# The gates' low parts multiplied on GpSimd instead of VectorE, with two buffers of the one-hots that it reads

## The chip, the cores and the metric

One core of one Trainium2 chip. The metric is the time of one execution on the device in microseconds, the median of several runs.

## The reference, cut to what matters

The program is a two-block transformer on 512 tokens of width 1024. The change lies in the first block's expert layer, `peer_ffn`: each token and head picks 16 of 128 x 128 = 16384 experts, each named by a pair of key numbers, and a softmax over the picks' scores gives gates.

```python
q = (xi @ w_q).reshape(n, PEER_HEADS, 2, PEER_KEY_DIM)
s = jnp.einsum('nhpc,hpkc->nhpk', q, sub_keys)
ts, ti = lax.top_k(s, PEER_TOPK)
...
idx = jnp.take_along_axis(cand_i, best_p, axis=-1)
gate = jax.nn.softmax(best_s, axis=-1)
act = gelu(jnp.einsum('nd,nhkd->nhk', xi, u[idx]))
return jnp.einsum('nhk,nhkd->nd', gate * act, v[idx])
```

## The kernel before, in words

Each engine has a program of its own (`TensorProgram`, `ScalarProgram`, `VectorProgram`, `PoolProgram` for GpSimd, `SyncProgram` for DMAs), written out by hand in the order in which the engine runs it. They meet through semaphores: `.up(...)` counts one up when an instruction has finished, `wait_ge(*signal.at(...))` waits for it. An engine does nothing else while it waits.

Of the 512 tokens, 384 (`DT`) go through the expert layer densely: TensorE multiplies them with all 16384 rows of `u` and of `v`, in 128 tiles of 128 experts, and a matrix of gates, zero for experts that a token did not pick, is multiplied in between. The other 128 tokens (one tile, `ROW_TILE`) are done by rows: for each of their 128 picks GpSimd asks for the picked row of `u` or `v` by an indirect DMA (`ask`, L2649 to L2660), into one of four slots (`ROW_SLOTS`), and VectorE takes the dot product (L2219) or adds the row to a sum (L2232); that is `VectorProgram.rows`, and it counts `row_used` up. There are 256 such requests, numbered i by `ROW_USES`; request i waits until row i - 4 is used.

Numbers of high precision are split into two bf16 parts, and TensorE multiplies high with high, low with high and high with low (L564 to L566). Blocks of weights (128x4096) are loaded by Sync, their high part is made by ScalarE (L1289) and their low part by VectorE (`low_part`, L2003) or, outside the expert layer's stretch, by GpSimd in pieces of 512 columns (L2565).

The matrix of gates is built in the loop of `gate_matrices`, 48 steps (`HOT_STEPS = DT // OC`) of 8 tokens each (`OC`), in two buffers by n % 2:

- VectorE (L2369 to L2393) makes the one-hots of the first key number, `one_hot_a` (L2385), and of the second, `one_hot_b` (L2388; one buffer). It multiplies the latter by the gates' high part (L2390) and low part (L2391) into `gated_one_hot_b` 0 and 1; the last counts `hot` up. All are bf16, 128x1024. Between steps it works on rows up to `ROWS_HOT[n]` (three rows in four steps) and on low parts of weights up to `LOWS_HOT[n]` (nine 128x4096 blocks between 849.5 and 1052 us). `one_hot_a` waits until TensorE has used its buffer (`gate_mats`, step n - 2).
- TensorE (L956 to L969) waits for `hot`, multiplies the one-hots (L967, 16 products of 128x128x128 per step), and then runs the dense tiles of `HOT_FILL[n]`, three in four steps, each of 24 products over 384 columns.
- ScalarE (L1603) copies the result (L1613), Sync stores it, and both serve the dense tiles between.
- GpSimd is in `ask` the whole time, ahead of the loop, through it and long after it; `run` calls it once, at L2606.

After the loop TensorE does 12 more dense tiles (`LAST_FILL`) and then the second half of the layer, `experts`.

Of the kernel before, what the change touches and what calls it, by code (L numbers as in the profile page):

```python
# [8 lines left out]
BF16 = mybir.dt.bfloat16  # L9
U32 = mybir.dt.uint32  # L10
ALU = mybir.AluOpType
# [3 lines left out]
P = 128  # L15
# [16 lines left out]
PH, NK, TOPK = 8, 128, 16  # L32
# [9 lines left out]
OC, OI = 8, 2  # L42

ROW_TILE, DT = QT - 1, SEQ - P
ROW_SLOTS = 4
# [41 lines left out]
class Signals:  # L87


    def __init__(self, nc, reached):  # L90
# [69 lines left out]
        self.hot = self.new("one_hots_ready")  # L160
# [42 lines left out]
class Layout:  # L203


    def __init__(self, nc, n_columns):
        m = Map(nc, nc.sbuf_base)
# [27 lines left out]
        m = Map(nc, after_gla)  # L235
        self.norm1 = NormBuffers(m, "norm1", T)
        self.h0 = m("tokens_in", [P, KT, T])
        m = Map(nc, after_gla)
        self.z, self.logit = m("z", [2 * GLA_RANK, T]), m("gate_logit", [P, 4, T])
        self.soft, self.ones_row = m("gate_soft", [P, 4, T]), m("ones_row", [P, T])  # L240
        m = Map(nc, free)
# [25 lines left out]
        self.left, self.right = hot("one_hot_a", one_hots, BF16), hot("one_hot_b", one_hots[:1] + one_hots[2:], BF16)  # L267
# [269 lines left out]
class TensorProgram:  # L537
# [418 lines left out]
    def gate_matrices(self):  # L956
        nc, s, k, m = self.nc, self.s, self.k, self.m
        for n in range(DT // OC):
            v = n % 2
            nc.tensor.wait_ge(*s.hot.at(n))  # L960
            for q in range(OC // 4):
                event = ("gate_mats", n, q)
                i = self.take(event, (s.act_out, event))
                for x in range(4):
                    for part in range(2):
                        c, y = divmod(4 * q + x, OI)
                        ins = nc.tensor.matmul(k.psum[:, i, NK * x:NK * (x + 1)], m.left[:, v, c, :, y],  # L967
                                               m.gated[part][:, v, c, :, y], start=part == 0, stop=part == 1)
                ins.then_inc(*s.gate_mats.up(n, q))  # L969
            self.fill(HOT_FILL[n])  # L970
# [832 lines left out]
class VectorProgram:  # L1803
# [565 lines left out]
    def gate_matrices(self):  # L2369
# [8 lines left out]
        for n in range(HOT_STEPS):  # L2378
            v, tokens = n % 2, slice(OC * n, OC * (n + 1))
            number_a, number_b, gate_high, gate_low = (  # L2380
                m.pick_b[:, x, tokens].rearrange("p (c n) -> p c n", n=OI).unsqueeze(2).to_broadcast(hots)
                for x in range(4))
# [3 lines left out]
            if n >= 1:  # L2386
                nc.vector.wait_ge(*s.hot.at(n - 1))
            nc.vector.tensor_tensor(m.right[:, :, :, :], iota, number_b, ALU.is_equal).then_inc(*s.step.up())  # L2388
            nc.vector.wait_ge(*s.step.now())
            nc.vector.tensor_tensor(m.gated[0][:, v], m.right[:, :, :, :], gate_high, ALU.mult).then_inc(*s.step.up())  # L2390
            nc.vector.tensor_tensor(m.gated[1][:, v], m.right[:, :, :, :], gate_low, ALU.mult).then_inc(*s.hot.up(n))  # L2391
# [160 lines left out]
class PoolProgram:  # L2552
# [19 lines left out]
    def run(self):  # L2572
# [33 lines left out]
        self.ask()  # L2606
# [42 lines left out]
    def ask(self):  # L2649
# [4 lines left out]
        for i, (kind, h, x) in enumerate(ROW_USES):  # L2654
# [241 lines left out]
```

## Time and profile before

| | |
|---|---|
| median of 3 runs | 2268.46 us (2267.76 to 2269.29) |
| profiled execution, its own time | 2262.53 us |
| its span | 2261.2 us |
| mean granted clock of TensorE | 0.972 of full |
| TensorE / VectorE / ScalarE / GpSimd busy | 2109.3 / 1524.8 / 890.9 / 713.0 us |
| GpSimd, 256 requests for rows | 80.5 + 100.4 + 95.6 + 93.6 us |
| GpSimd, weight splits L2565 | 299.5 us in 229 pieces |
| loop of gate matrices | 849.5 to 1052 us |

In the profile PE is TensorE, DVE VectorE, ACT ScalarE, POOL GpSimd and SP Sync. Times are microseconds, unless a column says ns. A group of instructions shows its busy time and the mean of one, then the idle time of its engine ahead of it and what ended that. A stretch shows how long each engine was busy in it, PEclk, the TensorE clock that was granted (1.00 is full speed, 0.50 half), the share of the DMA engines and what they moved. Records of one engine may overlap by their fixed ends, so the distance from start to start tells the pace better than a duration.

### The profile page before, as it was taken

Reading aid. Unit: us, or ns where it says so; the run is one execution under the profiler, and the core shown is the slowest. Engines: PE = TensorE matmul, PEld = TensorE weight load, DVE = VectorE, ACT = ScalarE, POOL = GpSimd, SP = SyncE. Lnnn points to the kernel's source line nnn. Section 1 sums busy time; section 2 is a strip of 40 time slices with the busy share of each in tenths; the row PEclk is TensorE's granted clock in tenths of the full one; section 3 lists DMA queues with packets and bytes.
Section 4 is the critical chain, followed back from the end, with each engine's and each line's share of the span. In section 5 each row is a group of like instructions: output and inputs, shape, how many; then the busy total and the mean of one; then the engine's idle time right before and its main releaser. Section 6 shows DMA issues by size and latency. Waiting matters only on the chain.

```text
span 2261.2 us, 31215 instructions
## 1 busy us (share of the span) xinstructions
PE 2109.3 (93%) x12667; PEld 1220.4 (54%) x12743; DVE 1524.8 (67%) x2558; ACT 890.9 (39%) x1066; POOL 713.0 (32%) x540
## 2 busy tenths in 40 slices
PE   6999889899999988999999999999789898999998
PEld 5464554455556646666665555555445464444444
DVE  4557664698889899998688888888674374432002
ACT  5333553333333336765433333333232454434110
POOL 2311001310333442232233333434336301555440
PEclk9999889999999999999999999999799998999999
DMA  5223552215988878899999999999422201322410
GB/s 207 75 75 114 197 203 83 84 49 195 330 307 299 333 274 300 332 353 341 372 373 378 376 382 377 382 382 374 174 75 98 75 20 38 112 83 104 149 38 37
DMA packets 194478, 483.37 MB, mean 214 GB/s; under 512 B 10672, under 2 KB 93648, under 8 KB 188320
## 3 DMA queue, kind: packets, MB, share of 16 engines
q1 hardware_dynamic: 154624, 334.65, 41.5%
q0 software_dynamic: 39712, 146.74, 17.2%
q8 instruction: 100, 1.64, 0.3%
q14 instruction: 42, 0.34, 0.0%
HBM read 428.92 MB, written 52.43 MB: 213 GB/s over the span
## 4 chain that ended last, share of the span: by engine, by line
PE 48%; DVE 29%; DMA 14%; issue 3%; ACT 3%; POOL 1%; SPq 1%; DVEq 0%; ACTq 0%; POOLq 0%
PE psum L565 13%; PE psum L566 13%; PE psum L564 13%; DMA expert_act<-act_dram 12%; DVE weight_low L2003 6%; DVE row_sum L2232 2%; POOL weight_low L2565 1%; DVE hidden_low L2411 1%; DVE gated_one_hot_b L2391 1%; DVE one_hot_b L2388 1%; DVE one_hot_a L2385 1%; DVE expert_act L2406 1%; DVE rows_a L2219 1%; PE psum L758 1%; PE psum L779 1%
## 5 line engine op out<-in xcount | busy, mean ns | idle before, releaser
L564 PE MATMUL psum<-x_high,weight_high 128*128 128x384 bf16 (+3 forms) x1826 | 630.0, 345 | 21.1 <-DVE weight_low L2003 15.7
L565 PE MATMUL psum<-x_low,weight_high 128*128 128x384 bf16 (+3 forms) x1845 | 637.2, 345 | 12.1 <-DVE x_low L1881 5.9
L566 PE MATMUL psum<-x_high,weight_low 128*128 128x384 bf16 (+3 forms) x1844 | 636.5, 345 | 0.6
L1289 ACT ACTIVATE weight_high<-weight_stage 128x4096 bf16<-128x4096 f32 (+2 forms) x100 | 356.3, 3564 | 240.8 <-PE psum L566 118.1
L2565 POOL TENSOR_TENSOR weight_low<-weight_stage,weight_high 128x512 bf16<-128x512 f32 (+1 forms) x229 | 299.5, 1341 | 422.7 <-ACT weight_high L1289 422.7
L564 PE MATMUL psum<-hidden_high,weight_high 128*128 128x384 bf16 x1024 | 333.8, 326 | 6.3 <-DVE hidden_low L2411 6.2
L566 PE MATMUL psum<-hidden_high,weight_low 128*128 128x384 bf16 x1024 | 333.8, 326 | 0.0
L565 PE MATMUL psum<-hidden_low,weight_high 128*128 128x384 bf16 x1024 | 333.8, 326 | 0.0
L2003 DVE TENSOR_TENSOR weight_low<-weight_stage,weight_high 128x4096 bf16<-128x4096 f32 x69 | 304.6, 4416 | 11.0 <-ACT weight_high L1289 11.0
L564 PEld LDWEIGHTS psum<-x_high,weight_high 128*128 128x128 bf16 (+1 forms) x1856 | 183.3, 99 | 183.1 <-issue 20.5
L566 PEld LDWEIGHTS psum<-x_high,weight_low 128*128 128x128 bf16 (+1 forms) x1856 | 183.4, 99 | 154.1 <-issue 7.0
L565 PEld LDWEIGHTS psum<-x_low,weight_high 128*128 128x128 bf16 (+1 forms) x1856 | 183.3, 99 | 144.4 <-issue 5.5
L1562 ACT ACTIVATE norm_value<-psum 128x384 f32<-128x384 f32 x128 | 62.1, 490 | 297.2 <-PE psum L566 225.0
L2659 POOL DMA_INDIRECT rows_a<-u_rows_dram,row_index x64 | 80.5, 1258 | 287.5 <-DVE rows_a L2219 195.5
L2659 POOL DMA_INDIRECT rows_b<-u_rows_dram,row_index x64 | 100.4, 1569 | 174.5 <-DVE rows_b L2219 168.1
L2659 POOL DMA_INDIRECT rows_b<-peer_v_dram,row_index x64 | 95.6, 1493 | 146.7 <-DVE row_sum L2232 131.8
L564 PEld LDWEIGHTS psum<-hidden_high,weight_high 128*128 128x128 bf16 x1024 | 100.1, 98 | 75.9 <-issue 9.5
L2659 POOL DMA_INDIRECT rows_a<-peer_v_dram,row_index x64 | 93.6, 1462 | 145.1 <-DVE row_sum L2232 135.3
L566 PEld LDWEIGHTS psum<-hidden_high,weight_low 128*128 128x128 bf16 x1024 | 100.2, 98 | 66.2
L565 PEld LDWEIGHTS psum<-hidden_low,weight_high 128*128 128x128 bf16 x1024 | 100.2, 98 | 64.5
L1633 ACT ACTIVATE hidden_high<-expert_act 128x384 bf16<-128x384 f32 x128 | 61.5, 522 | 160.2 <-DVE expert_act L2406 160.2
L2406 DVE TENSOR_TENSOR expert_act<-expert_act,gates 128x384 f32<-128x384 f32 x128 | 62.9, 553 | 74.8 <-DMA expert_act<-act_dram 74.8
(350 smaller groups left out, 2926.3 us busy)
## 6 DMA issues: line engine op xcount, KB each, us to landing
weight_stage<-peer_u_dram SPq DMA_DIRECT2D x32, 2048.0 KB
weight_stage<-peer_v_dram SPq DMA_DIRECT2D x32, 2048.0 KB
weight_stage<-mlp_w_dram SPq DMA_DIRECT2D x16, 2048.0 KB
weight_stage<-ada_w_dram SPq DMA_DIRECT2D x12, 2048.0 KB
act_dram<-norm_value SPq DMA_DIRECT2D x128, 192.0 KB
gate_dram<-gate_matrices SPq DMA_DIRECT2D x12, 2048.0 KB, 9.9
gates<-gate_dram SPq DMA_DIRECT2D x32, 768.0 KB
expert_act<-act_dram SPq DMA_DIRECT2D x32, 768.0 KB
```

The costliest lines, as they stand in the source:

```text
L564: self.nc.tensor.matmul(out, left[0], right[0], start=first, stop=False)
L565: self.nc.tensor.matmul(out, left[0], right[1], start=False, stop=False)
L566: return self.nc.tensor.matmul(out, left[1], right[0], start=False, stop=last)
L758: ins = nc.tensor.matmul(k.psum[strip, i, :], m.cond[:, t, :], rows[:, t, :], start=t < 4, stop=t >= 4)
L1289: nc.scalar.activation(k.block_view(m.w_high, n % SPLITS, n), k.block_view(m.w_stage, n % STAGES, n), ACT.Copy).then_inc(*s.w_high.up(n))
L1562: nc.scalar.activation(m.norm2.value[:, tile % 4, 0:DT], k.tile_bank(event, DT), ACT.Gelu).then_inc(*s.activated.up(*event))
L1633: nc.scalar.activation(m.hid_high[:, n % 2, b, :], m.act[:, n % 2, b, :], ACT.Copy).then_inc(*s.hid_high.up(n, b))
L2003: nc.vector.tensor_tensor(k.block_view(m.w_low, n % SPLITS, n), k.block_view(m.w_stage, n % STAGES, n), k.block_view(m.w_high, n % SPLITS, ...
L2232: nc.vector.scalar_tensor_tensor(m.row_sum[:, :], row, m.row_weight[:, at], m.row_sum[:, :], ALU.mult, ALU.add).then_inc(*s.row_used.up(i))
L2406: nc.vector.tensor_tensor(v, v, m.gates[:, n % 2, :, b, :], ALU.mult).then_inc(*s.gated.up(n, b))
L2565: ins = nc.gpsimd.tensor_tensor(m.w_low[:, n % SPLITS, at], m.w_stage[:, n % STAGES, at], m.w_high[:, n % SPLITS, at], ALU.subtract)
L2659: nc.gpsimd.indirect_dma_start(m.rows[i % ROW_SLOTS], None, v if layer else u, index).then_inc(*s.in_rows[i % ROW_SLOTS].up(i))
```

## The change

VectorE makes `one_hot_b` in two buffers and counts the new signal `right_hot` up; it no longer multiplies by the low part, and its product with the high part now counts `hot` up. GpSimd makes the product with the low part (`PoolProgram.gate_matrices`) and counts `gated_low` up. TensorE waits for both. VectorE waits for `gated_low` of step n - 2 before it writes `one_hot_b` again. GpSimd's requests are cut into parts: those up to `ROWS_ROUTE[-1] + 4` ahead of the loop, then after each product those up to `ROWS_HOT[n] + 3`, and the rest after the loop. In `Layout` the second buffer moves `gated_one_hot_b` and what lies behind it 2 KB per partition up.

```diff
--- before.py
+++ after.py
@@ -157,7 +157,8 @@
         self.softening = self.new("gates_softening")
         self.added = self.new("residual_added")
         self.routed = self.new("experts_chosen")
-        self.hot = self.new("one_hots_ready")
+        self.hot, self.right_hot = self.new("one_hots_ready"), self.new("one_hots_b_ready")
+        self.gated_low = self.new("gated_low_ready")
         self.rescaled = self.new("second_sums_scaled")
         self.summed = self.new("squares_added")
         self.gated = self.new("hidden_gated")
@@ -264,7 +265,7 @@
         self.tot = m("gate_sum", [P, 2, PH])
         hot = Map(nc, top)
         one_hots = [P, 2, OC // OI, NK, OI]
-        self.left, self.right = hot("one_hot_a", one_hots, BF16), hot("one_hot_b", one_hots[:1] + one_hots[2:], BF16)
+        self.left, self.right = hot("one_hot_a", one_hots, BF16), hot("one_hot_b", one_hots, BF16)
         self.gated = [hot(f"gated_one_hot_b_{part}", one_hots, BF16) for part in range(2)]
         mats = hot.at
         self.mats = hot("gate_matrices", [P, 2, NK, TC])
@@ -958,6 +959,7 @@
         for n in range(DT // OC):
             v = n % 2
             nc.tensor.wait_ge(*s.hot.at(n))
+            nc.tensor.wait_ge(*s.gated_low.at(n))
             for q in range(OC // 4):
                 event = ("gate_mats", n, q)
                 i = self.take(event, (s.act_out, event))
@@ -2377,18 +2379,17 @@
         iota = m.iota[:, :, :].unsqueeze(1).to_broadcast(hots)
         for n in range(HOT_STEPS):
             v, tokens = n % 2, slice(OC * n, OC * (n + 1))
-            number_a, number_b, gate_high, gate_low = (
+            number_a, number_b, gate_high = (
                 m.pick_b[:, x, tokens].rearrange("p (c n) -> p c n", n=OI).unsqueeze(2).to_broadcast(hots)
-                for x in range(4))
+                for x in range(3))
             if n >= 2:
                 nc.vector.wait_ge(*s.gate_mats.at(n - 2, OC // 4 - 1))
             nc.vector.tensor_tensor(m.left[:, v], iota, number_a, ALU.is_equal).then_inc(*s.step.up())
-            if n >= 1:
-                nc.vector.wait_ge(*s.hot.at(n - 1))
-            nc.vector.tensor_tensor(m.right[:, :, :, :], iota, number_b, ALU.is_equal).then_inc(*s.step.up())
-            nc.vector.wait_ge(*s.step.now())
-            nc.vector.tensor_tensor(m.gated[0][:, v], m.right[:, :, :, :], gate_high, ALU.mult).then_inc(*s.step.up())
-            nc.vector.tensor_tensor(m.gated[1][:, v], m.right[:, :, :, :], gate_low, ALU.mult).then_inc(*s.hot.up(n))
+            if n >= 2:
+                nc.vector.wait_ge(*s.gated_low.at(n - 2))
+            nc.vector.tensor_tensor(m.right[:, v], iota, number_b, ALU.is_equal).then_inc(*s.right_hot.up(n))
+            nc.vector.wait_ge(*s.right_hot.at(n))
+            nc.vector.tensor_tensor(m.gated[0][:, v], m.right[:, v], gate_high, ALU.mult).then_inc(*s.hot.up(n))
             self.rows(ROWS_HOT[n])
             self.low_parts(LOWS_HOT[n])
 
@@ -2603,7 +2604,7 @@
         nc.gpsimd.dma_start(m.iota32[:, :], d["iota_keys"]).then_inc(*s.in_iota_keys.up())
         for g in range(4):
             self.begin(("peer_q", g))
-        self.ask()
+        self.gate_matrices()
         self.begin(("v", NG - 1))
 
         nc.gpsimd.wait_ge(*s.added.at("experts", KT - 1))
@@ -2646,12 +2647,32 @@
                                 rv[:, :, mid:mid + 1].to_broadcast([P, SEQ // n, n]), ALU.subtract).then_inc(
             *s.gla_step.up(i))
 
-    def ask(self):
+    def gate_matrices(self):
+
+        nc, s, m = self.nc, self.s, self.m
+        asked = ROWS_ROUTE[-1] + ROW_SLOTS
+        self.ask(0, asked)
+        nc.gpsimd.wait_ge(*s.routed.at("split", ROUTE_TILES[-1]))
+        for n in range(HOT_STEPS):
+            v, tokens = n % 2, slice(OC * n, OC * (n + 1))
+            gate_low = m.pick_b[:, 3, tokens].rearrange("p (c n) -> p c n", n=OI).unsqueeze(2).to_broadcast(
+                [P, OC // OI, NK, OI])
+            nc.gpsimd.wait_ge(*s.right_hot.at(n))
+            if n >= 2:
+                nc.gpsimd.wait_ge(*s.gate_mats.at(n - 2, OC // 4 - 1))
+            nc.gpsimd.tensor_tensor(m.gated[1][:, v], m.right[:, v], gate_low, ALU.mult).then_inc(*s.gated_low.up(n))
+            until = ROWS_HOT[n] + ROW_SLOTS - 1
+            self.ask(asked, until)
+            asked = max(asked, until)
+        self.ask(asked, len(ROW_USES))
+
+    def ask(self, first, end):
 
         nc, s, k, m = self.nc, self.s, self.k, self.m
         u, v = k.d["u_rows"], k.d["peer_v"].rearrange("b a n -> (b a) n")
         nc.gpsimd.wait_ge(*s.routed.at("row_lists"))
-        for i, (kind, h, x) in enumerate(ROW_USES):
+        for i in range(first, end):
+            kind, h, x = ROW_USES[i]
             pick, layer = TOPK * h + x, int(kind == "sum")
             if i >= ROW_SLOTS:
                 nc.gpsimd.wait_ge(*s.row_used.at(i - ROW_SLOTS))
```

## Rows read from the trace of the kernel before

**Rows 1.** The page: the span, and the engines' busy time, share and instructions.
```profile
span 2261.2 us, 31215 instructions
...
PE 2109.3 (93%) x12667; PEld 1220.4 (54%) x12743; DVE 1524.8 (67%) x2558; ACT 890.9 (39%) x1066; POOL 713.0 (32%) x540
```

**Rows 2.** Busy time of each engine by stretch; the first column is its length.
```profile
core 0: us, PE busy (x) PEld busy (x) DVE busy (x) ACT busy (x) POOL busy (x), PEclk, DMA share, GB/s
...
900.00:950.00 50.00, 47.05 (x412) 32.20 (x411) 49.60 (x62) 34.43 (x37) 17.35 (x9) 1.00 0.91 350
...
1052.00:1100.00 48.00, 48.00 (x300) 28.96 (x298) 25.58 (x21) 19.64 (x21) 11.50 (x7) 1.00 0.95 340
1100.00:1600.00 500.00, 493.72 (x3032) 295.71 (x3030) 422.41 (x481) 174.12 (x162) 193.92 (x141) 1.00 1.03 373
...
849.50:1052.00 202.50, 185.04 (x1607) 127.86 (x1608) 198.40 (x256) 137.16 (x140) 56.05 (x36) 0.98 0.89 334
```

**Rows 3.** Groups of instructions, 849.5 to 1052 us: busy, mean ns | idle before.
```profile
L967 PE MATMUL psum<-gated_one_hot_b,one_hot_a 128*128 128x128 bf16 x767 | 53.0, 223 | 18.7 <-DVE gated_one_hot_b L2391 18.7
...
L2003 DVE TENSOR_TENSOR weight_low<-weight_stage,weight_high 128x4096 bf16<-128x4096 f32 x9 | 39.8, 4419 | 0.0
...
L2388 DVE TENSOR_TENSOR one_hot_b<-iota_bf,picks_t_bf 128x1024 bf16<-128x1024 bf16 x48 | 33.2, 691 | 0.0
...
L2391 DVE TENSOR_TENSOR gated_one_hot_b<-one_hot_b,picks_t_bf 128x1024 bf16<-128x1024 bf16 x48 | 32.8, 684 | 0.0
...
L2232 DVE SCALAR_TENSOR_TENSOR row_sum<-rows_a,modulation_rows,row_sum 128x1024 f32<-128x1024 f32 x9 | 11.5, 1279 | 0.0
```

**Rows 4.** Timeline, the first products of the loop on TensorE.
```profile
852.21 1.89 PE L967 MATMUL psum<-gated_one_hot_b,one_hot_a 128*128 128x128 bf16 x16 [3.96 <-DVE gated_one_hot_b L2391]
```

**Rows 5.** Timeline of VectorE, the low product and what follows it: start, us, instruction.
```profile
880.14 0.69 DVE L2391 TENSOR_TENSOR gated_one_hot_b<-one_hot_b,picks_t_bf 128x1024 bf16<-128x1024 bf16 x1
880.74 4.42 DVE L2003 TENSOR_TENSOR weight_low<-weight_stage,weight_high 128x4096 bf16<-128x4096 f32 x1
```

**Rows 6.** The view of line L2391: ns min/median/max, first and last start.
```profile
L2391 DVE TENSOR_TENSOR gated_one_hot_b<-one_hot_b,picks_t_bf x48: 682/684/686, 851.5 to 1049.3; 128x1024 bf16<-128x1024 bf16 x48
```

**Rows 7.** Timeline of GpSimd and of VectorE beside it, 420 us.
```profile
420.12 8.96 POOL L2565 TENSOR_TENSOR weight_low<-weight_stage,weight_high 128x512 bf16<-128x512 f32 x8 [5.25 <-ACT weight_high L1289]
...
422.46 0.29 DVE L2198 MAX8 best_side<-scores 128x8 f32<-128x128 f32 x1 [6.88 <-ACT scores L1585]
```

**Rows 8.** Timelines in the loop: GpSimd's requests, and VectorE beside the last.
```profile
896.52 1.15 POOL L2659 DMA_INDIRECT rows_a<-u_rows_dram,row_index  x1 [2.53 <-DVE rows_a L2219]
902.78 4.88 POOL L2659 DMA_INDIRECT rows_a<-peer_v_dram,row_index  x1 [5.12 <-DVE row_sum L2232]
...
902.43 4.42 DVE L2003 TENSOR_TENSOR weight_low<-weight_stage,weight_high 128x4096 bf16<-128x4096 f32 x1
```

**Rows 9.** Timelines of GpSimd and VectorE, the convolution.
```profile
1675.00 12.65 POOL L2565 TENSOR_TENSOR weight_low<-weight_stage,weight_high 128x512 bf16<-128x512 f32 x8 [25.94 <-ACT weight_high L1289]
...
1701.03 28.45 POOL L2565 TENSOR_TENSOR weight_low<-weight_stage,weight_high 128x512 bf16<-128x512 f32 x8 [1.68 <-ACT weight_high L1289]
...
1701.03 20.65 POOL L2565 TENSOR_TENSOR weight_low<-weight_stage,weight_high 128x512 bf16<-128x512 f32 x1 [1.68 <-ACT weight_high L1289]
...
1699.39 21.28 DVE L2441 SCALAR_TENSOR_TENSOR norm_square<-conv_padded,columns,norm_square 128x512 f32<-128x512 f32 x32
```

**Rows 10.** The MLP: GpSimd's timeline for one block; the view of VectorE's L2540.
```profile
1938.46 10.75 POOL L2565 TENSOR_TENSOR weight_low<-weight_stage,weight_high 128x512 bf16<-128x512 f32 x8 [7.16 <-ACT weight_high L1289]
...
L2540 DVE TENSOR_TENSOR norm_square<-norm_square x32: 692/1216/1642, 1922.5 to 2078.6; 128x512 f32<-128x512 f32 x32
```

**Rows 11.** Busy time by stretch, TensorE alone: length, busy, granted clock, DMA share, GB/s.
```profile
255.00:300.00 45.00, 36.78 (x237) 0.92 0.61 210
...
1860.00:1911.00 51.00, 40.50 (x257) 0.89 0.12 42
1624.00:1648.00 24.00, 18.27 (x76) 0.72 0.38 156
```

## The prediction

> **What bounds the kernel now.** The page comes first. TensorE is busy for 93% of the span, VectorE for 67%, GpSimd for 32% [rows 1]; such averages do not say what the touched loop waits for. The busy time by stretch does: in the loop of gate matrices (849.5 to 1052 us) VectorE is busy 198.40 of 202.50 us, and 49.60 of 50 in a stretch of its middle, TensorE only 185.04 and 47.05 [rows 2]. So there VectorE sets the pace. After it the roles change: TensorE is busy 48.00 of 48 us and then 493.72 of 500, VectorE 25.58 and 422.41 [rows 2]. Time lost or won by TensorE in the loop is therefore not made up later; it reaches the end whole, but for some 6 us.
>
> The groups of the loop [rows 3] show the work of its 48 steps: four bf16 operations over 128x1024 per step, 36 expert rows (1.2 to 1.3 us), 9 splits of weights (4.42 us). TensorE sat idle 18.7 us, all of it for the product with the low parts, L2391, and 3.96 us of that ahead of the first step [rows 3, 4]. That leaves 14.7 us: the most that any relief of VectorE can give.
>
> VectorE's timeline gives the price of one operation on the path [rows 5]: L2391 starts at 880.14 and its follower at 880.74, so 0.60 us, not the 0.69 of its record. The 48 runs of L2391 start between 851.5 and 1049.3 us [rows 6], so a step takes VectorE 197.8 / 47 = 4.21 us.
>
> **The change part by part.**
> (1) VectorE drops 48 of L2391: 48 x 0.60 = 28.8 us less.
> (2) GpSimd gains 48 two-input products over 1024 columns. No row has it with bf16 on both sides. Its nearest row is its own weight split, two inputs, 512 columns: 8 in 8.96 us, 1.12 each, while VectorE ran MAX8 and the like, with one tensor input [rows 7]. Twice the columns: 2.24 us. Bounds: 1.12, if two bf16 inputs go at twice the rate, and 2.8, if the gates' repeated pairs and a cold start of every single piece cost a quarter more. I take 2.24, since the row is the same operation. The 36 requests in the loop take GpSimd 56.05 us [rows 2], mostly 1.15 each [rows 8]. 48 x 2.24 + 56 = 164 of 202 us: as a sum of its own it fits.
> (3) What decides is whether GpSimd's product can run beside VectorE. Nearly all that VectorE does in the loop reads two tensors from SBUF (all groups of VectorE in [rows 3], and the product with the high part like its twin L2391). Three places show such work meeting GpSimd's. In the convolution VectorE's 32 L2441 alone take 21.28 us, 0.665 each, and a GpSimd piece that came amid them ended after 20.65 us, when they were through; the same 8 pieces took 28.45 us [rows 9]. A little earlier 8 pieces and VectorE's stream took turns: 12.65 us, 1.58 per piece [rows 9]. In the MLP, 8 pieces take 10.75 us in place of 8.96, and VectorE's L2540, a product of two inputs, goes from 0.69 to a median of 1.22 and up to 1.64 us [rows 10]. In the loop itself a request of GpSimd took 4.88 us, not 1.15, when it came at 902.78 in a weight split of 4.42 us that had begun at 902.43 [rows 8]. So the two take turns. One turn costs 1.58 where VectorE's alone costs 0.665: GpSimd's piece of 1.12 adds 0.915, all but 0.2.
> Then one product adds 2.24 - 0.2 = 2.04 us to VectorE's step and takes 0.60 away: 4.21 + 1.44 = 5.65 us. **Sum: 48 x 1.44 = +69 us.**
> The Trainium skill (SBUF — State Buffer, SBUF: two separate sides) calls the shared port pair an exclusive lock that the winner keeps for its whole instruction; nothing would then overlap, and the sum would be 48 x 1.64 = +79 us. I keep the 0.2 that the alternating rows show.
> (4) The second buffer of one_hot_b takes away VectorE's wait for its own product; that never cost anything here (L2388 shows 0.0 idle [rows 3]). In its place L2388 waits for GpSimd's product of two steps before, and behind it in VectorE's queue stand the product with the high part, which TensorE needs, the rows and the splits. If GpSimd is kept out while VectorE streams, as in the 20.65 us case, this wait and that of one_hot_a for TensorE are what stop VectorE, at most two steps ahead; GpSimd goes in, TensorE takes its 16 products (53.0 / 48 = 1.1 us [rows 3]), and the count per step is again the two engines' work one after the other. So whoever wins the port, the sum is nearly the same; if GpSimd waits for VectorE to stop, some of its product lies beside that stop, and I take 3 us off for the whole loop.
> (5) Requests for rows now stand behind the products. At step n GpSimd asks up to ROWS_HOT[n] + 3, three rows beyond those that VectorE works on in that step, so four steps ahead (three rows per four steps): 4 x 5.6 = 22 us less a lag of up to two steps, 11 us. The wait for a used row is always met by then. A request of 1.15 us and a transfer must fit in 11 us; requests come at 0.75 per step with 3.4 us free for them, so I cost it at nothing. If it is late VectorE idles, and GpSimd's next product goes under that idle time.
> (6) TensorE's new wait for the low product: it is the same product as before, only by another engine. TensorE needs 185.04 us for the loop [rows 2] of the new 270, so it is covered; ScalarE (137 us) also.
> (7) The buffer shifts the tiles behind it by 2 KB per partition; no transfer or operation changes size. Nothing.
>
> The profiled execution took 2262.53 us, 5.9 under the median of 2268.46; the difference is applied to the median: 2268.5 + 69 - 3 = 2334.5, with 2 us for a clock that drops more often (below): **2336 us**.
>
> **Rivals.**
> *A, the loop becomes TensorE's, faster.* If bf16 operations leave GpSimd its port, its product runs beside one-hots and only the rows (36 x 1.2) and splits (9 x 4.4) hold it off, 83 of 202 us, and it needs 108 of the rest. VectorE then needs 4.21 - 0.60 = 3.61 us a step, 173 in all, TensorE 185, so TensorE bounds: 12 to 14 us off, 2255 us. Against it: nothing in the rows shows GpSimd at full rate beside a two-input operation of VectorE. For it: all three collisions are with f32 inputs, none with bf16 on both sides. The Trainium skill (Advanced Engine Details and Errata, VectorE Performance Modes) gives the 16-bit mode "1 read port", which, read alone, would give this rival's time; no row here tests it. Chance 0.10. It decides when GpSimd's product beside bf16 one-hots lasts about 2.3 us and VectorE's stay at 0.69.
> *B, partly so.* Some of the products fall into stops of VectorE, or GpSimd's bf16 rate is double: 4.21 - 0.60 + 1.12 - 0.2 = 4.53 us, 48 x 0.32 = +15 us, 2284. Between A and B lies a mix that gives no change. Chance 0.10 for B and the way to the main case, 0.04 for no change.
> *C, more is lost.* TensorE's granted clock: in this trace it was 0.72 in a stretch with 18.27 of 24 us busy, 0.89 with 40.50 of 51, 0.92 with 36.78 of 45 [rows 11]. In the new loop TensorE is busy 185 / 48 = 3.85 of 5.65 us, 68%. At the lower level (1.2 of 2.4 GHz) its step takes 7.7 us, over VectorE's 5.65, so each microsecond at that level loses 0.27. At a mean clock of 0.85, a little under the last two of these, 30% of 270 us lie at that level, some 80, and 80 x 0.27 = +22 us; the high bound of GpSimd's product adds 48 x 0.56 = 27. Alone 2358 or 2363, together 2385. Chance 0.16.
>
> **Numbers.** The main case, 2320 to 2350, has 0.60. The range reaches down to B at 2284 and up to both of C, 2385; A and no change, 0.14, stay outside, and about 0.05 beyond its ends. No change means within 0.2% (4.5 us), about what a measurement of this kernel can tell. Faster 0.10, same 0.04, slower 0.86.
>
> **What would show it.** Right: the loop from first one-hot to last is 260 to 280 us, VectorE and GpSimd together fill it; GpSimd's 48 products have a mean well over 2.24 us, or some VectorE one-hots last 2 to 3 us in place of 0.69; TensorE waits more than 60 us for the low product or for VectorE's high one; everything behind the loop keeps its length. Wrong: products of 2.3 us with one-hots of 0.69 beside them (A); a loop under 200 us; row transfers at the head of VectorE's waits (then step 5 fails); TensorE busy nearly all of the loop at half clock (C).

## The result, and the profile after

The changed kernel takes 2317.93 us (median of 4 runs, 2317.17 to 2318.87) against 2268.58 before: 49.3 us more, a ratio of 1.0216 with an interval of 1.02 to 1.0232. The forecast was 2336 us, in a range of 2284 to 2385.

The profiled execution took 2318.24 us, its span is 2317.0. It is compared with the other one by stretches, since the profiled execution of before lay 5.9 us under its median, and 4 us of that difference lie ahead of the loop (its first one-hot starts at 849.5 there and 853.5 here).

The busy time by stretch, with the same columns as in [rows 2]:

```profile
core 0: us, PE busy (x) PEld busy (x) DVE busy (x) ACT busy (x) POOL busy (x), PEclk, DMA share, GB/s
853.50:1106.00 252.50, 202.35 (x1609) 136.81 (x1610) 250.37 (x208) 137.05 (x140) 176.80 (x84) 0.88 0.74 270
...
1106.00:1155.00 49.00, 49.00 (x305) 29.53 (x303) 26.21 (x22) 19.46 (x21) 10.04 (x7) 1.00 0.94 335
1155.00:1655.00 500.00, 491.53 (x3017) 294.18 (x3016) 419.40 (x480) 174.01 (x162) 194.01 (x141) 1.00 1.03 372
```

VectorE is busy 250.37 of 252.50 us: it still sets the pace of the loop, with fewer instructions (208, not 256) that last longer. TensorE was busy 185.04 of 202.50 us before, now 202.35 of 252.50, at a mean clock of 0.88 in place of 0.98. Behind the loop everything keeps its length: from TensorE's last product of the loop to the end it is 1209.0 us before and 1210.8 now, with TensorE busy in 49.00 of the first 49 us and in 491.53 of the next 500 (493.72 before).

The view of `one_hot_a` shows the loop's length from its first and last start, before and after:

```profile
L2385 DVE TENSOR_TENSOR one_hot_a<-iota_bf,picks_t_bf x48: 681/685/694, 849.5 to 1047.4; 128x1024 bf16<-128x1024 bf16 x48
```

```profile
L2387 DVE TENSOR_TENSOR one_hot_a<-iota_bf,picks_t_bf x48: 676/680/2381, 853.5 to 1098.9; 128x1024 bf16<-128x1024 bf16 x48
```

(1098.9 - 853.5) / 47 = 5.22 us a step, against 4.21; 47 x 1.01 = 47.5 us. Of the 49.3 us all but some 2, the size of what moves between executions, are here.

The groups of the loop, with the columns of [rows 3]. First one of before, which is L2221 in the changed kernel, then those of the changed kernel:

```profile
L2219 DVE SCALAR_TENSOR_TENSOR rows_b<-rows_b,normed_rows 128x1024 f32<-128x1024 f32 x9 | 11.0, 1219 | 0.0
```

```profile
L2663 POOL TENSOR_TENSOR gated_one_hot_b<-one_hot_b,picks_t_bf 128x1024 bf16<-128x1024 bf16 x48 | 114.2, 2380 | 72.3 <-DVE one_hot_b L2390 64.2 <-issue 8.2
...
L969 PE MATMUL psum<-gated_one_hot_b,one_hot_a 128*128 128x128 bf16 x768 | 59.5, 236 | 51.4 <-issue 51.4
...
L2387 DVE TENSOR_TENSOR one_hot_a<-iota_bf,picks_t_bf 128x1024 bf16<-128x1024 bf16 x48 | 47.3, 985 | 0.5 <-PE psum L969 0.4
L2005 DVE TENSOR_TENSOR weight_low<-weight_stage,weight_high 128x4096 bf16<-128x4096 f32 x9 | 44.8, 4980 | 0.0
L2392 DVE TENSOR_TENSOR gated_one_hot_b<-one_hot_b,picks_t_bf 128x1024 bf16<-128x1024 bf16 x48 | 33.2, 692 | 1.7
...
L2390 DVE TENSOR_TENSOR one_hot_b<-iota_bf,picks_t_bf 128x1024 bf16<-128x1024 bf16 x48 | 32.5, 678 | 0.0
...
L2221 DVE SCALAR_TENSOR_TENSOR rows_b<-rows_b,normed_rows 128x1024 f32<-128x1024 f32 x9 | 26.2, 2916 | 0.0
L2234 DVE SCALAR_TENSOR_TENSOR row_sum<-rows_b,modulation_rows,row_sum 128x1024 f32<-128x1024 f32 x9 | 26.2, 2915 | 0.0
...
L2680 POOL DMA_INDIRECT rows_a<-u_rows_dram,row_index x9 | 15.2, 1691 | 1.4 <-issue 0.9
```

What VectorE does right behind its product with the high part grew: the expert rows from 1.22 and 1.28 to 2.92 us (one group of nine to a mean of 2.74), one_hot_a from 0.69 to a mean of 0.99, the splits from 4.42 to a mean of 4.98. one_hot_b and the high product kept 0.68 and 0.69. The timelines of both engines over two steps show why. GpSimd:

```profile
885.98 2.40 POOL L2663 TENSOR_TENSOR gated_one_hot_b<-one_hot_b,picks_t_bf 128x1024 bf16<-128x1024 bf16 x1 [0.45 <-DVE one_hot_b L2390]
888.53 1.78 POOL L2680 DMA_INDIRECT rows_a<-u_rows_dram,row_index  x1 [0.15 <-issue]
890.74 2.40 POOL L2663 TENSOR_TENSOR gated_one_hot_b<-one_hot_b,picks_t_bf 128x1024 bf16<-128x1024 bf16 x1 [0.43 <-DVE one_hot_b L2390]
```

VectorE beside it:

```profile
885.93 0.69 DVE L2392 TENSOR_TENSOR gated_one_hot_b<-one_hot_b,picks_t_bf 128x1024 bf16<-128x1024 bf16 x1
886.54 2.91 DVE L2234 SCALAR_TENSOR_TENSOR row_sum<-rows_a,modulation_rows,row_sum 128x1024 f32<-128x1024 f32 x1
889.38 0.68 DVE L2387 TENSOR_TENSOR one_hot_a<-iota_bf,picks_t_bf 128x1024 bf16<-128x1024 bf16 x1
889.98 0.68 DVE L2390 TENSOR_TENSOR one_hot_b<-iota_bf,picks_t_bf 128x1024 bf16<-128x1024 bf16 x1
890.70 0.69 DVE L2392 TENSOR_TENSOR gated_one_hot_b<-one_hot_b,picks_t_bf 128x1024 bf16<-128x1024 bf16 x1
891.30 6.12 DVE L2005 TENSOR_TENSOR weight_low<-weight_stage,weight_high 128x4096 bf16<-128x4096 f32 x1
```

GpSimd's product starts 0.05 us after VectorE's product with the high part (the high product, from here on), at 885.98, and ends at 888.38. VectorE's row starts at 886.54 on time, and lasts 2.91 in place of 1.28; the split after the next product lasts 6.12 in place of 4.42. Wherever the operation behind the high product is a one-hot, a row or a split, it is longer by 1.63 to 1.70 us, once per step. Added up over the loop, VectorE's groups grew by 14.4 (one_hot_a), 5.0 (splits), 15.2, 14.7, 15.2 and 13.2 (rows, with those of 11.0, 11.5, 11.0 and 11.5 us before) and 1.7 (the row weights' small product): 79 us, of which the dropped L2391 gives back 28.8. That is 51, less the 2 us for which VectorE no longer waits for TensorE. From here on the hold is the time by which GpSimd's operation makes one of VectorE's longer.

### The profile page after: what moved, and what is told of

Its sections match the earlier page's. It is cut to its first block, busy times and chain, and to the rows that moved or that the text cites. A ratio compares the mean times of both kernels' runs of the same rounds, so it can differ in the third digit from the quotient of the medians.

```text
span 2317.0 us, 31299 instructions
## 1 busy us (share of the span) xinstructions
PE 2131.1 (92%) x12667; PEld 1232.8 (53%) x12743; DVE 1574.1 (68%) x2510; ACT 890.4 (38%) x1066; POOL 832.8 (36%) x588
## 4 chain that ended last, share of the span: by engine, by line
PE 46%; DVE 31%; DMA 14%; issue 4%; ACT 3%; POOL 1%; SPq 1%; DVEq 0%; ACTq 0%; POOLq 0%
PE psum L566 12%; DMA expert_act<-act_dram 12%; PE psum L567 12%; PE psum L565 12%; DVE weight_low L2005 7%; DVE row_sum L2234 4%; DVE one_hot_a L2387 2%; DVE rows_a L2221 2%; DVE rows_b L2221 2%; DVE hidden_low L2412 1%; POOL weight_low L2566 1%; DVE one_hot_b L2390 1%; PE psum L759 1%; DVE expert_act L2407 1%; PE psum L780 1%
## 5 line engine op out<-in xcount | busy, mean ns | idle before, releaser
L2005 DVE TENSOR_TENSOR weight_low<-weight_stage,weight_high 128x4096 bf16<-128x4096 f32 x69 | 309.6, 4488 | 12.6 <-ACT weight_high L1291 12.6
L2680 POOL DMA_INDIRECT rows_a<-u_rows_dram,row_index x64 | 85.9, 1343 | 256.0 <-DVE rows_a L2221 162.8
L2680 POOL DMA_INDIRECT rows_b<-peer_v_dram,row_index x64 | 100.3, 1567 | 115.4 <-DVE row_sum L2234 98.9
L2663 POOL TENSOR_TENSOR gated_one_hot_b<-one_hot_b,picks_t_bf 128x1024 bf16<-128x1024 bf16 x48 | 114.2, 2380 | 72.3 <-DVE one_hot_b L2390 64.2
```

Of the source, the lines that this page charges most:

```text
L2005: nc.vector.tensor_tensor(k.block_view(m.w_low, n % SPLITS, n), k.block_view(m.w_stage, n % STAGES, n), k.block_view(m.w_high, n % SPLITS, ...
L2663: nc.gpsimd.tensor_tensor(m.gated[1][:, v], m.right[:, v], gate_low, ALU.mult).then_inc(*s.gated_low.up(n))
L2680: nc.gpsimd.indirect_dma_start(m.rows[i % ROW_SLOTS], None, v if layer else u, index).then_inc(*s.in_rows[i % ROW_SLOTS].up(i))
```

## The experiments

In all of them the code that isn't named is that of the changed kernel, if not said otherwise. "Before" is the kernel before, run on the same chip in the same session.

### The collision, or the new waits?

**Both products back on VectorE, with two buffers and all the new signals.**

```diff
-            nc.gpsimd.tensor_tensor(m.gated[1][:, v], m.right[:, v], gate_low, ALU.mult).then_inc(*s.gated_low.up(n))
+            nc.vector.tensor_tensor(m.gated[1][:, v], m.right[:, v], gate_low, ALU.mult).then_inc(*s.gated_low.up(n))
```

> Both products are VectorE's again; the two buffers of one_hot_b, the new signals and the cut-up requests stay. Theory T (GpSimd's product and VectorE's two-input operations take turns, 1.70 us of VectorE's time per product): the time of before, 2268 us within 5, the loop 198 us from first to last one-hot. Rival W (the new waits and the requests that stand behind them cost the time, not the product's collision): it stays slow, 2300 us or more.

Measured: 2268.41 us, ratio to before 0.9997 (0.9982 to 1.0012). The loop is as long as before:

```profile
L2387 DVE TENSOR_TENSOR one_hot_a<-iota_bf,picks_t_bf x48: 680/685/694, 850.6 to 1048.9; 128x1024 bf16<-128x1024 bf16 x48
```

(1048.9 - 850.6) / 47 = 4.22 us a step. The second buffer, the cut-up requests and GpSimd's waits cost nothing; W is out. So the time comes with the product on GpSimd.

**No product with the low parts at all.**

```diff
-            nc.gpsimd.tensor_tensor(m.gated[1][:, v], m.right[:, v], gate_low, ALU.mult).then_inc(*s.gated_low.up(n))
...
-            nc.tensor.wait_ge(*s.gated_low.at(n))
...
-            if n >= 2:
-                nc.vector.wait_ge(*s.gated_low.at(n - 2))
...
-m.gated[part][:, v, c, :, y]
+m.gated[0][:, v, c, :, y]
```

> The product with the gates' low parts is left out; TensorE reads the high part in its place, so its work is unchanged. This is what the change would bring if GpSimd's product cost VectorE nothing. T: VectorE's step falls by 0.60 us, TensorE becomes the bound after some 12 us: 2254 to 2258 us. W: the waits that are left (GpSimd still waits for one_hot_b and TensorE's products ahead of its requests) keep it above 2268.

Measured: 2249.83 us, ratio 0.992 (0.9901 to 0.9939), so 18 us less, with an interval of 14 to 22. What a free product would bring:

```profile
L968 PE MATMUL psum<-gated_one_hot_b,one_hot_a 128*128 128x128 bf16 x768 | 51.7, 222 | 3.6 <-DVE gated_one_hot_b L2389 3.6
...
L2386 DVE TENSOR_TENSOR one_hot_a<-iota_bf,picks_t_bf 128x1024 bf16<-128x1024 bf16 x48 | 33.0, 687 | 13.4 <-PE psum L968 13.3
```

VectorE now waits for TensorE (13.4 us ahead of one_hot_a), and TensorE's products of the one-hots wait only 3.6 us for VectorE, against 18.7 in [rows 3]: the bound has changed over, as T has it. The gain is somewhat more than expected (2254 to 2258 us).

### What of GpSimd's work collides?

**A memset in place of the product (the low parts are left out).**

```diff
-            nc.gpsimd.tensor_tensor(m.gated[1][:, v], m.right[:, v], gate_low, ALU.mult).then_inc(*s.gated_low.up(n))
+            nc.gpsimd.memset(m.gated[1][:, v], 0.0).then_inc(*s.gated_low.up(n))
```

> GpSimd fills gated_one_hot_b 1 with zeros in place of the product: it writes as much and reads nothing from SBUF. T, in the form that two-input reads of both engines collide: VectorE's operations keep 0.69, 1.22, 1.28 and 4.42 us and the time is that of e2_no_low, about 2256. Rival: any operation of GpSimd on SBUF holds VectorE off, then the operation behind the high product is still longer by the memset's length less 0.6 us and the time lies over 2270.

Measured: 2255.51 us in one run, while runs of before in that session lay between 2263.5 and 2273.3. GpSimd writes the same tile, at the same place in the step; GpSimd's and VectorE's timelines:

```profile
880.06 0.95 POOL L2663 MEMSET gated_one_hot_b<- 128x1024 bf16 x1 [0.46 <-DVE one_hot_b L2390]
...
883.19 0.95 POOL L2663 MEMSET gated_one_hot_b<- 128x1024 bf16 x1 [0.45 <-DVE one_hot_b L2390]
```

```profile
880.03 0.69 DVE L2392 TENSOR_TENSOR gated_one_hot_b<-one_hot_b,picks_t_bf 128x1024 bf16<-128x1024 bf16 x1
880.64 1.28 DVE L2234 SCALAR_TENSOR_TENSOR row_sum<-rows_a,modulation_rows,row_sum 128x1024 f32<-128x1024 f32 x1
...
883.16 0.69 DVE L2392 TENSOR_TENSOR gated_one_hot_b<-one_hot_b,picks_t_bf 128x1024 bf16<-128x1024 bf16 x1
883.77 4.42 DVE L2005 TENSOR_TENSOR weight_low<-weight_stage,weight_high 128x4096 bf16<-128x4096 f32 x1
```

The row beside the memset takes 1.28 us, the split 4.42: not a hundredth more than in [rows 3]. The loop, 854.3 to 1036.1 us from first to last `one_hot_a`, is within a microsecond of that without any product (853.8 to 1034.7). So it isn't GpSimd's work on SBUF as such.

**A copy in place of the product: one input (the low parts are left out here too).**

```diff
+            nc.gpsimd.tensor_copy(m.gated[1][:, v], m.right[:, v]).then_inc(*s.gated_low.up(n))
```

> GpSimd copies one_hot_b (one input) in place of the product, which leaves the gates' low parts out. T in the form that any read by GpSimd collides: VectorE's operation behind the high product is longer by the copy's length less 0.5 us, at some 1 us for the copy +0.5 us a step, the time about 2268 - 29 + 24 + 5 = 2268. Rival: only two-input products collide, then the time is that of the memset, 2255, and VectorE's operations keep their length.

Measured: 2277.84 us in one run; before 2267.14. VectorE's timeline:

```profile
882.15 0.69 DVE L2392 TENSOR_TENSOR gated_one_hot_b<-one_hot_b,picks_t_bf 128x1024 bf16<-128x1024 bf16 x1
882.76 2.06 DVE L2234 SCALAR_TENSOR_TENSOR row_sum<-rows_a,modulation_rows,row_sum 128x1024 f32<-128x1024 f32 x1
...
886.05 0.69 DVE L2392 TENSOR_TENSOR gated_one_hot_b<-one_hot_b,picks_t_bf 128x1024 bf16<-128x1024 bf16 x1
886.67 5.25 DVE L2005 TENSOR_TENSOR weight_low<-weight_stage,weight_high 128x4096 bf16<-128x4096 f32 x1
```

The row takes 2.06 us, 0.78 more than alone; the split 5.25, 0.83 more. A single read by GpSimd collides as well, and the rival (only two-input products) is out. The hold of about 0.8 us gives 48 x (0.8 - 0.6) = +10, near the 10.7 of this one run. The expectation of no change took 0.5 us off a copy of 1 us; the copy's record is 1.55 us with its wait, and it holds VectorE off for 0.8. The memset writes the same tile and reads nothing, the copy reads and writes: what collides is GpSimd's reading. The Trainium skill (SBUF — State Buffer, SBUF: two separate sides) has it so, that VectorE's operation with two SBUF inputs contends "only against a GpSimd op that reads SBUF"; the trace agrees, with 0.00 us for the memset and 0.8 for the copy.

### How long is the hold?

**GpSimd's product with VectorE idle.**

```diff
-            nc.vector.wait_ge(*s.right_hot.at(n))
+            nc.vector.wait_ge(*s.gated_low.at(n))
             nc.vector.tensor_tensor(m.gated[0][:, v], m.right[:, v], gate_high, ALU.mult).then_inc(*s.hot.up(n))
```

> VectorE's product with the high part waits for GpSimd's product, so GpSimd's runs with VectorE idle. If the 2.40 us record of the change's product holds a wait of 0.6 us for VectorE's high product, it now takes 1.8 us; if it computed beside that product all along, it stays at 2.3 to 2.4 us. In the second case the step is 4.21 - 0.60 + 2.6 = 6.2 us and the time some 2268 + 48 x 2.0 = 2365; in the first some 2340.

Measured: 2330.87 us in one run. The view of the product's line:

```profile
L2663 POOL TENSOR_TENSOR gated_one_hot_b<-one_hot_b,picks_t_bf x48: 1892/1892/1895, 855.8 to 1115.9; 128x1024 bf16<-128x1024 bf16 x48
```

1.89 us, in all 48. So in the changed kernel 0.5 of its 2.40 us was a wait for VectorE's high product to end, the first of the two cases. Then it held VectorE off for 1.70. (VectorE waited 97.1 us for it in the loop; less the 28.8 of the dropped product that makes 2337 us, 6 over what was measured in this one run.)

**The half of it.** GpSimd takes 512 columns, VectorE the other 512.

```diff
-            nc.gpsimd.tensor_tensor(m.gated[1][:, v], m.right[:, v], gate_low, ALU.mult)...
+            nc.vector.tensor_tensor(m.gated[1][:, v, 2:4], m.right[:, v, 2:4], gate_low[:, 2:4], ALU.mult)...
+            nc.gpsimd.tensor_tensor(m.gated[1][:, v, 0:2], m.right[:, v, 0:2], gate_low[:, 0:2], ALU.mult)...
```

> GpSimd multiplies the first 512 of the 1024 columns, VectorE the other 512. T (VectorE is held off for as long as GpSimd's product runs, less what lies beside the high product): GpSimd's hold falls from 1.70 to about 0.85 us, and VectorE does 0.34 us of the 0.60 itself: 48 x (0.85 + 0.34 - 0.60) = +28 us on before, about 2297. Rival F (most of a collision is a fixed price, whatever the size): +48 x (1.7 - 0.26) = +69, 2337.

Measured: 2293.91 us, 27 more than before's 2267.14; ratio 1.0124 (1.0108 to 1.0139), so 24 to 32 us, with the expected 28 inside; F is out. GpSimd's record fell from 2.40 to 1.54 us, and VectorE's half of the product, which now stands behind the high product, takes the hold:

```profile
L2664 POOL TENSOR_TENSOR gated_one_hot_b<-one_hot_b,picks_t_bf x48: 1471/1542/1544, 850.2 to 1073.8; 128x512 bf16<-128x512 bf16 x48
...
L2393 DVE TENSOR_TENSOR gated_one_hot_b<-one_hot_b,picks_t_bf x48: 1259/1260/1264, 850.7 to 1074.3; 128x512 bf16<-128x512 bf16 x48
```

So 512 columns of GpSimd's product cost 0.86 us and a product some 0.17 besides (1.89 - 2 x 0.86).

**Twice.** GpSimd makes the same product a second time.

```diff
+            nc.gpsimd.tensor_tensor(m.gated[1][:, v], m.right[:, v], gate_low, ALU.mult).then_inc(*s.gated_twice.up(n))
+            nc.gpsimd.wait_ge(*s.gated_twice.at(n))
             nc.gpsimd.tensor_tensor(m.gated[1][:, v], m.right[:, v], gate_low, ALU.mult).then_inc(*s.gated_low.up(n))
```

> GpSimd makes its product twice, the second when the first has ended. T: VectorE is held off once more per step, by the 1.7 to 1.9 us of the second product: 2318 + 48 x 1.8 = 2404 us. Rival: if VectorE's operations got in ahead of the second and GpSimd only fell behind, the two-step buffers take it up and the time stays under 2360.

Measured: 2393.55 us in one run, 75.6 more than the changed kernel, 1.58 a step, near T's 2404 and far over 2360. VectorE's timeline has both holds now, in two bf16 one-hots that follow each other:

```profile
878.71 2.38 DVE L2388 TENSOR_TENSOR one_hot_a<-iota_bf,picks_t_bf 128x1024 bf16<-128x1024 bf16 x1
881.01 2.38 DVE L2391 TENSOR_TENSOR one_hot_b<-iota_bf,picks_t_bf 128x1024 bf16<-128x1024 bf16 x1
883.43 0.69 DVE L2393 TENSOR_TENSOR gated_one_hot_b<-one_hot_b,picks_t_bf 128x1024 bf16<-128x1024 bf16 x1
```

Each is longer by 1.70 us. The loop itself grew by a little less, 1.66 a step (first and last `one_hot_a` at 852.1 and 1175.3 us). These are also the clearest rows against rival A: an operation with bf16 on both sides is held off as long as the f32 rows are.

**The price that the forecast took, 1.12 us for 512 columns.** The kernel before, with the splits' pieces at 1024 columns.

```diff
-STAGES, SPLITS, BLOCK, PIECE = 2, 3, 4096, 512
+STAGES, SPLITS, BLOCK, PIECE = 2, 3, 4096, 1024
```

> The kernel before, with GpSimd's weight splits in pieces of 1024 columns in place of 512; it prices what the forecast took from them (2 x 1.12 = 2.24 us for 1024 columns). If the 2.24 against 1.89 us alone was a fixed price counted twice, a block of 4096 columns at a quiet place takes 8.96 - 4 x 0.17 = 8.3 us or less, 2.0 to 2.1 a piece; if two bf16 inputs are simply quicker than f32 with bf16, it stays at 8.8 to 9.0 us, 2.2 a piece. The time of the kernel stays within 5 us of before.

Measured: 2267.22 us in one run (before 2264.96). GpSimd's timeline at the same block as in [rows 7]:

```profile
422.13 8.38 POOL L2565 TENSOR_TENSOR weight_low<-weight_stage,weight_high 128x1024 bf16<-128x1024 f32 x4 [5.25 <-ACT weight_high L1289]
```

8.38 in place of 8.96 us: 2.09 per 1024 columns, against 2.24 for two pieces of 512. So a piece has a price of its own of 0.58 / 4 = 0.15 us, near what the half product showed, and doubling the row of 512 counted it twice. But that is less than half of the gap to the 1.89 us of the product alone. The first two of these four pieces:

```profile
422.13 4.21 POOL L2565 TENSOR_TENSOR weight_low<-weight_stage,weight_high 128x1024 bf16<-128x1024 f32 x2 [5.25 <-ACT weight_high L1289]
```

Each further piece adds (8.38 - 4.21) / 2 = 2.09 us, so the first, which followed idle time, took 2.12 by itself, and 1.89 is 0.23 less. GpSimd's product of two bf16 inputs is thus quicker than its subtraction of bf16 from f32, by a tenth. Whether that comes from the type of the inputs, from the operation or from the repeated pairs of the gates no run separates. Both answers that the expectation named hold in part.

### Does the place matter?

**GpSimd waits for the high product.**

```diff
-            nc.gpsimd.wait_ge(*s.right_hot.at(n))
+            nc.gpsimd.wait_ge(*s.hot.at(n))
```

> GpSimd's product waits for VectorE's high product (hot) in place of one_hot_b, so it asks for the port when the operation behind the high product has already begun. T (each product costs VectorE the 1.70 us that the port is held, wherever it falls): the same 2318 us within 5, with the delay moved one operation on, and GpSimd's record longer by up to a row or split. Rival S (a late GpSimd is kept out while VectorE's operations follow one another, as in the convolution's 20.65 us): records of 5 us and more, VectorE stops at its waits for gated_low and gate_mats, and the time lies over 2325.

Measured: 2320.25 us, ratio 1.0235 (1.0206 to 1.0264), the same as the changed kernel's 1.0216 within the intervals. GpSimd's and VectorE's timelines:

```profile
887.61 2.87 POOL L2663 TENSOR_TENSOR gated_one_hot_b<-one_hot_b,picks_t_bf 128x1024 bf16<-128x1024 bf16 x1 [0.56 <-DVE gated_one_hot_b L2392]
890.62 1.25 POOL L2680 DMA_INDIRECT rows_a<-u_rows_dram,row_index  x1 [0.15 <-issue]
892.43 6.00 POOL L2663 TENSOR_TENSOR gated_one_hot_b<-one_hot_b,picks_t_bf 128x1024 bf16<-128x1024 bf16 x1 [0.56 <-DVE gated_one_hot_b L2392]
```

```profile
887.44 1.28 DVE L2234 SCALAR_TENSOR_TENSOR row_sum<-rows_a,modulation_rows,row_sum 128x1024 f32<-128x1024 f32 x1
888.64 2.38 DVE L2387 TENSOR_TENSOR one_hot_a<-iota_bf,picks_t_bf 128x1024 bf16<-128x1024 bf16 x1
...
891.65 0.69 DVE L2392 TENSOR_TENSOR gated_one_hot_b<-one_hot_b,picks_t_bf 128x1024 bf16<-128x1024 bf16 x1
892.26 4.42 DVE L2005 TENSOR_TENSOR weight_low<-weight_stage,weight_high 128x4096 bf16<-128x4096 f32 x1
896.60 2.38 DVE L2387 TENSOR_TENSOR one_hot_a<-iota_bf,picks_t_bf 128x1024 bf16<-128x1024 bf16 x1
```

The product of 887.61 comes when the row of 887.44 has begun, so it is the one that waits, 2.87 us in all, and the one-hot behind the row takes the delay. The product of 892.43 stands behind a split of 4.42 us for 6.00, and gets in at once when the split is over. It was never kept out over several operations: of its 48 records three are of 6.00 us, each behind a split, and the others last at most 2.87. But VectorE does stop here, as S had it, for TensorE and not for `gated_low`:

```profile
L2387 DVE TENSOR_TENSOR one_hot_a<-iota_bf,picks_t_bf 128x1024 bf16<-128x1024 bf16 x48 | 78.7, 1640 | 19.7 <-PE psum L969 19.6
```

Part of the cost has moved from longer records into these 19.6 us (0.4 in the changed kernel); seven products last 1.89 us, as with VectorE idle. The time is still that of the changed kernel, and not over S's 2325: S is out for this loop. That GpSimd can be kept out for longer the convolution showed [rows 9]; what sets it off was not tried.

### Both one-hots in one operation, both products in another

What VectorE can save in the loop without another engine's read: the kernel before, with both one-hots in one operation of 2048 columns and both products in another. For the access patterns to fit, the picks are laid out by steps.

```diff
-        self.iota16, self.pick_b = m("iota_picks", [P, TOPK]), m("picks_t_bf16", [P, 4, DT], BF16)
+        self.iota16, self.pick_b = m("iota_picks", [P, TOPK]), m("picks_t_bf16", [P, DT // OC, 4, OC], BF16)
...
-            nc.vector.tensor_tensor(m.left[:, v], iota, number_a, ALU.is_equal).then_inc(*s.step.up())
-            nc.vector.tensor_tensor(m.right[:, :, :, :], iota, number_b, ALU.is_equal).then_inc(*s.step.up())
+            nc.vector.tensor_tensor(m.both[:, v], iota, numbers, ALU.is_equal).then_inc(*s.step.up())
...
-            nc.vector.tensor_tensor(m.gated[0][:, v], m.right[:, :, :, :], gate_high, ALU.mult).then_inc(*s.step.up())
-            nc.vector.tensor_tensor(m.gated[1][:, v], m.right[:, :, :, :], gate_low, ALU.mult).then_inc(*s.hot.up(n))
+            nc.vector.tensor_tensor(m.gated[:, v].rearrange("p (x c) k n -> p x (c k n)", x=2), right,
+                                    gates, ALU.mult).then_inc(*s.hot.up(n))
```

> From the kernel before, GpSimd left out of it: VectorE makes both one-hots in one operation of 2048 columns and both products in another (the picks are laid out by steps for it), 2 instructions a step in place of 4. If each saved start is worth the 0.07 us between a 0.60 us spacing and 1024 columns at two a cycle (0.53), a step falls by 0.15 to 0.2 us and the loop by 7 to 9, of which TensorE's 14.7 us of idle time lets nearly all through: 2260 to 2263 us. If the larger pattern falls to one column a cycle (the 128x2048 place_one_hot takes 2.29 us), a step grows by 2 us and the time is 2360.

Measured: 2261.71 us, ratio to before 0.9977 (0.9968 to 0.9986), 5 us less: small, but beyond its interval, and the fastest of the three versions that leave nothing out. The groups of the two operations:

```profile
L2389 DVE TENSOR_TENSOR gated_one_hots<-one_hots_ab,picks_t_bf 128x2048 bf16<-128x2048 bf16 x48 | 58.8, 1225 | 1.6
L2385 DVE TENSOR_TENSOR one_hots_ab<-iota_bf,picks_t_bf 128x2048 bf16<-128x2048 bf16 x48 | 58.6, 1221 | 4.9 <-PE psum L966 4.3
```

1.22 us for 2048 columns, twice the 0.60 to 0.61 of the operations of 1024: the larger patterns keep the rate of the smaller. The one-hots start between 848.9 and 1042.8 us, 4.13 us a step, so only 0.08 of the 0.15 to 0.2 us came. Of before, the four operations took 0.60 + 0.61 + 0.72 + 0.60 = 2.53 us from start to start, now two take 2.4.

## Why the prediction was right, and where its size was off

**What bounds the loop: right.** VectorE before, VectorE after (250.37 of 252.50 us); a lengthening of the loop by 47.5 us reached the end as 49.3. That relief could bring at most 14.7 us holds within the noise: with the product gone 18 us came, interval 14 to 22, and TensorE's idle time ahead of the one-hots' products fell by 15.1.

**Step 1, 28.8 us less: right.** L2391 is gone, and VectorE's start-to-start distances elsewhere are unchanged.

**Step 3, that the two engines take turns: right**, for bf16 as for f32, and the 0.2 us of overlap is as forecast: 1.89 us alone, 1.70 of hold, 0.19 beside VectorE. The full lock of the Trainium skill (SBUF — State Buffer, SBUF: two separate sides) would give a hold of 1.89 and 9 us more; the trace shows 1.70, so VectorE is held off for nearly the whole operation, not quite all of it.

**Step 2 was mis-sized, and it is nearly the whole error.** The product was put at 2 x 1.12 = 2.24 us; it takes 1.89. Some 0.15 of the 0.35 is the price of each piece, doubled with the columns (1024 columns in one piece: 2.09). The other 0.20 is that GpSimd's product of two bf16 inputs is quicker than its subtraction from f32 was in a piece of the same size; the row had another type and another operation, and why it is slower stays open. With 1.89 - 0.19 = 1.70 the forecast's own sum reads 48 x (1.70 - 0.60) = 53 us in place of 69. That takes 16 of the 18 us between 2336 and 2317.93; the rest is within what moves between executions.

**Step 4: harmless, but argued with a wrong picture.** VectorE never stopped for `gated_low` or, but for 0.4 us, for TensorE: GpSimd, which asked 0.05 us after the high product had begun, got the next turn. The 3 us taken off for products under such stops had no ground here; in the run where GpSimd waits for the high product there were such stops, and they made the kernel no faster.

**Step 5, requests that stand behind products: right.** They mostly last 1.78 us instead of 1.15, and VectorE nowhere waits for a row's transfer in the loop. **Steps 6 and 7: right**, by the run with two buffers (0.9997).

**The rivals.** A is out as to its mechanism: the bf16 one-hot takes 2.38 us under GpSimd's product. The "1 read port" that the Trainium skill gives for the 16-bit mode (Advanced Engine Details and Errata, VectorE Performance Modes) would, read alone, have left it at 0.69; here the measurement decides. Its price was right in kind: with a memset, which doesn't collide, the kernel takes 2255.5 in one run, the 2255 of the forecast, and with no product at all 2249.8. B's double rate didn't show. C came in part: the granted clock of the loop fell from 0.98 to 0.88, near the 0.85 of that rival, and it cost nothing that can be seen. TensorE was busy 202 of 252 us with it, 4.2 us of each step of 5.2, and VectorE waited for it 0.4 us; the 7.7 us a step that the rival works out for the lower level never bound the loop. The 2 us set down for it were not needed.

**What would show it.** The loop took 245 us, not 260 to 280, which follows from step 2. TensorE waited 51.4 us, not over 60; here the lower clock counts too, since TensorE was busy 17 us longer for the same work (202.35, not 185.04). The mean of GpSimd's product (2.38 us) and the one-hots of 2.38 us were as described.

## What to carry to other kernels

In this loop, where VectorE runs operations with two SBUF inputs back to back, a GpSimd operation that reads SBUF costs VectorE nearly its own length. So work moved off a VectorE that sets the pace pays only if GpSimd's operation is shorter than the one it replaces (here 1.70 us of hold against 0.60), or falls where VectorE stops for good reason or reads one input (beside the pieces of [rows 7] VectorE's MAX8 keeps the 0.28 to 0.30 us that it takes without them); GpSimd's memset could stand beside it. When a price is taken from a row of many small pieces, split it into what grows with the columns and what each piece costs, and treat a row of another operation or type as a bound, not as the price.

## What the runs showed of the hardware that was not expected

- A copy by GpSimd, one bf16 input of 1024 columns, lasts some 1.04 us without its wait (1.55 less 0.5) and holds VectorE off for 0.8; a memset of the same tile lasts 0.95 us and holds it off for 0.00.
- The wait shows on either engine as a longer record, not as idle time: 2.91 us for a row of 1.28, 6.00 for a product of 1.89. The chain and the waits name no one for it, so only the comparison of durations finds it.
- A request of GpSimd ends some 0.9 us after the VectorE operation that it began in, however long that still lasts: 0.92 to 0.93 us after it for 25 of the 26 requests between 852 and 1045 us of the changed kernel, 0.89 to 0.94 us for 32 of 33 there before. So a request takes 1.78 us behind a product, in a held-off row, 0.98 in the run with the half product, where VectorE's operation was nearly over, and 4.88 in a split [rows 8]. VectorE did not grow by it.
- GpSimd's product of 1024 columns takes 1.89 us with two bf16 inputs; its subtraction of bf16 from f32 takes 2.12 alone and 2.09 from start to start. The cause of the difference was not tried.
